# Decay rows spread from DRAM, turned Gram products, sample states as the moving operand and state increments on four row groups

## The chip, the cores and the metric

The kernel runs on one core of one Trainium2 chip. The metric is the device time of one execution in microseconds (us), as the median of several runs. All data is float32.

## What is computed

One inference step of one decoder layer: 256 prompt tokens and 8 sample sequences of 4 tokens (288 tokens in all, model width 2048). RMSNorm, one input projection, two mixers side by side, one output projection, a mixture of 32 experts with top-2 choice, and a gated per-layer embedding. The change lies in mixer B, a gated DeltaNet with 8 heads of width 128. Per head, cut to what matters:

```python
G = jnp.cumsum(g, axis=-1)                                   # log decays, inside a chunk
decay = jnp.exp(jnp.where(causal, G[..., :, None] - G[..., None, :], -jnp.inf))
a_mat = jnp.where(strict, (k * beta[..., None]) @ k.T * decay, 0.0)
m = a_mat + eye                                              # unit lower triangular
u = solve(m, v * beta[..., None]); w = solve(m, k * beta[..., None] * exp(G)[..., None])
qk = q @ k.T * decay
v_new = u - w @ S
o = (q * exp(G)[..., None]) @ S + qk @ v_new
S = S * exp(G[-1]) + (k * exp(G[-1:] - G)[..., None]).T @ v_new
```

Every sample sequence has its own state S (128 x 128) for each head, so 8 of them per head; the outputs hold the new states too.

## The kernel before

The work is written out by hand for each engine, with semaphores between them. A prologue normalises and turns x (hT holds the 288 tokens as columns), then TensorE runs the first four pieces of the input projection and the sums behind the decays (L664 to L688). Then comes the loop over the heads (`head`, in the blocks of SyncE at L396, TensorE at L690, ScalarE at L1287 and VectorE at L1670): seven passes of a loop and a last one written out. After it come the output projection (L841 on), the experts, and the per-layer embedding.

In each head TensorE does two kinds of work. One is the chain of mixer B and of mixer A: turn v of mixer A, turn the old convolution rows (L712) and the new ones (L716), the sums of squares of q and k (L724), turn k and v and multiply q and k with themselves (`tok_mm`, L729 to L740), turn A and the q-k product (L746 to L750), six doubling levels of the triangular inverse (L753 to L788), u and w (L791 to L796), the states (L801 to L806), v_new (L810 to L812), the outputs (L815 to L819), the state increments of the samples (L823 to L825) and the sum of squares of the output (L827). The other kind is filler: `next_head()` puts the next head's input projection in between (96 matmuls of 128 weights by 288 columns), in portions that the list `FILL` fixes by hand, so that TensorE works while VectorE and ScalarE handle the chain. The last head has less filler (`LAST_FILL`): two pieces, and then the first matmuls of the output projection.

In the trace a float32 matmul stands as two MATMUL rows (two passes), and a transpose as one. A form such as 128*32 128x288 is 128 rows by 32 columns of weights, with 288 moving columns.

VectorE builds gcol (L1680), the decay differences dd (L1717), the masked decays DS and DC (L1724 to L1727), Am and QKm (L1730 to L1735), and from the turned Am fourteen masked blocks NT (L1745). It also does the convolution (L1690, L1694), the level updates (L1764 to L1767), eight masked copies Vm of the samples' v_new (L1804) and the new sample states (L1816). ScalarE takes the exponentials (L1323 to L1325), nine scaled copies of k and v (L1328 to L1330) and the copies out of PSUM. SyncE's queue carries all loads and stores of the heads: pieces of 1 MB, small rows per head, the states.

The products of the samples with their states: the state is the stationary operand and eight columns (w and q of one sequence) move past it, eight times per head.

Of the kernel before, what the change touches and what calls it, by code (L numbers as in the profile page):

```python
# [9 lines left out]
ALU = mybir.AluOpType  # L10
# [42 lines left out]
def _constants():  # L53
# [3 lines left out]
    same = (row // SEQ_LEN) == (col // SEQ_LEN)  # L57
    parts = [("ident", row == col), ("triu", row <= col), ("before", row < col), ("ones", row >= 0 * col),
             ("causal", row >= col), ("strict", row > col),
             ("low0", (row % 2 == 1) & (col == row - 1))]  # L60
    for lev in range(LEVELS):
# [5 lines left out]
              ("seq", row // SEQ_LEN == np.arange(SEQS)[None, :]),  # L67
# [46 lines left out]
def trunk(nc, d, o):  # L114

    ctx = ExitStack()
    with ctx:
# [77 lines left out]
        Dm = w(2, P)
        Ds = w(SAMPLE)
        DS = w(2, P)
        DSs = w(SAMPLE)
        eG = w(TOK)
        qg = w(TOK)  # L200
        Am = w(2, P)
        Ams = w(SAMPLE)
        QKm = w(2, P)
        QKms = w(SAMPLE)
# [10 lines left out]
        XTs = w(SAMPLE)  # L215
# [4 lines left out]
        uTs = w(SAMPLE)  # L220
        WQ = w(SEQS, 2 * SEQ_LEN)
# [3 lines left out]
        vnTs = w(SAMPLE)  # L225
        vns = w(P)
        Vm = w(SEQS, P)
# [3 lines left out]
        csT = w(3, P)  # L231
        stt = w(3, P)
# [15 lines left out]
        DC = w(2, P)  # L248
        DCs = w(SAMPLE)
# [49 lines left out]
        def gate_sig(q, t):  # L299
            if t == 2:  # L300
# [15 lines left out]
                 "tok_cp", "A_r", "AT_mm", "QKT_r", "NT_r", "W_r", "dS_mm", "W_T", "WT_r", "Wrep", "WTs_r", "ln_d",  # L316
                 "ln_sq", "vn_r", "mixA_mm", "mixA_r", "uw_mm", "uw_cp", "WQ_r", "S1_mm", "S1_r", "SQ_mm", "wS_mm",
                 "vn1_r", "vnT_r", "vnTT", "Vm_r", "vns_r", "o_mm", "S2_r", "Sn_r", "os_p", "os_r", "osq_r", "oss_mm", "rn_r", "or_r",
# [34 lines left out]
        def _(sp):  # L353
# [12 lines left out]
            def load_state(cols):  # L366
                for s in range(3):
                    sp.dma_start(stt[0:SEQS * PAD, s, :], conv_in[:, bass.ds(cols[s], P)]).then_inc(E["st_ld"], 16)
# [11 lines left out]

            for s in range(PIECES):
                load_piece(s, piece_col[s])
# [13 lines left out]
            def head(h, pieces, inputs):  # L396
# [19 lines left out]
                for s in range(3):  # L416
                    sp.dma_start(cv_p[:, bass.ds(c[s], P)], csT[0:PAD, s, :]).then_inc(E["cs_st"], 16)
                    sp.dma_start(cv_s[:, bass.ds(c[s], P)], csT[PAD:PAD + SEQS * PAD, s, :]).then_inc(E["cs_st"], 16)
# [161 lines left out]
        def _(pe):  # L580
# [106 lines left out]
            mm(ps[0:SAMPLE, 3, 16:24], C("btriu", SAMPLE), g[0:SAMPLE, 2, :])  # L687
            mm(ps[0:SAMPLE, 3, 40:48], C("ball", SAMPLE), g[0:SAMPLE, 2, :]).then_inc(dec["prep_mm"], 1)  # L688

            def head(h, fill):  # L690
# [38 lines left out]
                for t, (off, n) in enumerate(TILES):  # L729
                    pe.transpose(ps[0:n, 5, t * P:(t + 1) * P], qk[:, 1, off:off + n], C("ident"))  # L730
                    pe.transpose(ps[0:n, 6, t * P:(t + 1) * P], qkvT[:, 2, off:off + n], C("ident"))  # L731
                for t in range(2):
                    kt, qt = qk[:, 1, t * P:(t + 1) * P], qk[:, 0, t * P:(t + 1) * P]
# [3 lines left out]
                kt, qt = qk[:, 1, PROMPT:TOK], qk[:, 0, PROMPT:TOK]  # L737
                mm(ps[0:SAMPLE, 4, 0:SAMPLE], kt, kt)
                mm(ps[0:SAMPLE, 4, SAMPLE:2 * SAMPLE], qt, kt)
# [1354 lines left out]
```

## Time and profile before

| | |
|---|---|
| median of 3 runs | 1909.12 us (1908.06 to 1911.35) |
| profiled execution | 1911.12 us, span 1909.3 us |
| TensorE busy (matmul) | 1800.0 us, 94% |
| VectorE busy | 556.5 us, 29% |
| ScalarE busy | 388.0 us, 20% |
| mean DMA rate over the span | 278 GB/s |
| one pass of the head loop | 71.69 us |

The span is the time between the first and the last instruction of the profiled execution; the 1.8 us beside it are launch and end. Busy is time in which an engine executed an instruction. The heads take from 67 us to about 645 us. From about 810 us on the DMA engines move some 427 GB/s with almost no break, until 1740 us.

### The profile page before, as it was taken

How to read it: one execution, taken by the hardware profiler on the slowest of the kernel's cores; microseconds unless marked ns; L12 is line 12 of the kernel's file. 1: busy time of each engine (PE TensorE's matmuls, PEld its weight loads, DVE VectorE, ACT ScalarE, POOL GpSimd, SP SyncE). 2: the span in 40 equal slices, each digit the busy share in tenths (PEclk: the TensorE clock that was granted, in tenths of full speed). 3: DMA queues.
4: the chain of work that ended last, by engine and by line, in shares of the span. 5: the costliest groups of instructions: out<-in, count | busy, mean ns of one | idle time of the engine just before them, and what ended most of it. 6: DMA issues, size and time to landing. Idle time of an engine off the chain costs nothing.

```text
span 1909.3 us, 22816 instructions
## 1 busy us (share of the span) xinstructions
PE 1800.0 (94%) x8060; PEld 933.9 (49%) x8060; DVE 556.5 (29%) x1811; ACT 388.0 (20%) x922; POOL 19.5 (1%) x37
## 2 busy tenths in 40 slices
PE   7999999999998999999999999999999999999998
PEld 4777777777775433433333333333333333334333
DVE  2334434434434200321323213232132311224113
ACT  1424524524523111311000111001010010002103
POOL 0000000000000000000000000000000000000000
PEclk9999999999999999999999999999999999999999
DMA  8333433433404461599999999999999999999401
GB/s 253 100 95 102 126 94 103 124 94 104 124 28 149 152 250 73 199 419 428 427 428 427 427 427 427 427 427 427 428 426 427 425 427 425 424 424 384 168 22 50
DMA packets 208462, 519.92 MB, mean 272 GB/s; under 512 B 18664, under 2 KB 139488, under 8 KB 157152
## 3 DMA queue, kind: packets, MB, share of 16 engines
q1 hardware_dynamic: 198160, 513.83, 69.0%
q0 software_dynamic: 2304, 4.86, 0.7%
q10 hardware_dynamic: 7968, 0.83, 0.3%
q8 instruction: 19, 0.31, 0.1%
q14 instruction: 11, 0.09, 0.0%
HBM read 519.14 MB, written 12.26 MB: 278 GB/s over the span
## 4 chain that ended last, share of the span: by engine, by line
PE 79%; DMA 17%; DVE 2%; ACT 1%; issue 1%; SPq 0%; DVEq 0%; ACTq 0%
PE ps L582 75%; DMA ring<-in_w_down_dram 17%; PE ps L585 3%; DMA x<-in_x_sample_dram 0%; PE ps L1082 0%; ACT hb L1210 0%; ACT ring L1210 0%; SPq L477 0%; DMA pp_rows<-hb 0%; DVE ring L1694 0%; PE ps L710 0%; PE ps L730 0%; DVE ring L1745 0%; PE ps L731 0%; DVE x L2011 0%
## 5 line engine op out<-in xcount | busy, mean ns | idle before, releaser
L582 PE MATMUL ps<-ring,hT 128*64 128x512 f32 x2048 | 457.0, 596 | 25.6 <-DMA ring<-in_w_up_dram 25.6
L582 PE MATMUL ps<-hT,ring 128*128 128x288 f32 x1536 | 410.1, 414 | 0.0
L582 PE MATMUL ps<-ring,mixT 128*64 128x512 f32 (+2 forms) x1408 | 365.6, 598 | 35.9 <-DMA ring<-in_w_down_dram 25.6
L582 PEld LDWEIGHTS ps<-hT,ring 128*128 128x128 f32 x1536 | 283.3, 192 | 70.4 <-issue 0.5
L582 PEld LDWEIGHTS ps<-ring,hT 128*64 128x64 f32 x2048 | 145.7, 137 | 308.4 <-issue 305.8
L582 PEld LDWEIGHTS ps<-ring,mixT 128*64 128x64 f32 (+2 forms) x1408 | 124.8, 144 | 240.2 <-issue 238.3
L582 PE MATMUL ps<-ring,hb 128*128 128x512 f32 (+2 forms) x512 | 143.7, 512 | 0.0
L582 PE MATMUL ps<-mixT,wpT 128*128 128x512 f32 (+1 forms) x384 | 130.1, 601 | 0.0
L582 PEld LDWEIGHTS ps<-ring 128*128 128x128 f32 (+3 forms) x880 | 115.7, 186 | 29.0 <-DVE ring L1767 7.9
L582 PE MATMUL ps<-ring 128*128 128x128 f32 (+3 forms) x880 | 123.8, 272 | 1.7 <-DVE ring L1754 1.6
L1210 ACT ACTIVATE ring<-ps 128x256 f32<-128x256 f32 (+5 forms) x176 | 47.5, 310 | 294.4 <-PE ps L582 256.8
L582 PEld LDWEIGHTS ps<-ring,hb 128*128 128x128 f32 (+1 forms) x512 | 65.2, 170 | 78.1 <-issue 78.0
L1210 ACT ACTIVATE hT<-ps 128x512 f32<-128x512 f32 (+1 forms) x76 | 37.5, 494 | 322.6 <-PE ps L582 237.0
L2007 DVE TENSOR_TENSOR x<-x,ps 128x512 f32<-128x512 f32 x128 | 88.0, 687 | 24.8 <-PE ps L582 23.2
L1958 DVE TENSOR_SCALAR hT<-ps,gJ 128x128 f32<-128x128 f32 x128 | 35.9, 343 | 194.4 <-PE ps L585 194.4
L582 PEld LDWEIGHTS ps<-mixT,wpT 128*128 128x128 f32 (+1 forms) x384 | 49.8, 162 | 78.7 <-issue 53.6
L1999 DVE COPY mixT<-ps 128x512 f32<-128x512 f32 x16 | 11.1, 691 | 215.4 <-PE ps L582 215.4
L1210 ACT ACTIVATE wpT<-ps 128x288 f32<-128x288 f32 (+2 forms) x19 | 7.2, 383 | 318.4 <-PE ps L1082 313.9
L1210 ACT ACTIVATE mixT<-ps 128x512 f32<-128x512 f32 x32 | 19.1, 597 | 223.7 <-PE ps L582 223.7
L1210 ACT ACT_TABLE_LOAD x47 | 60.3, 1283 | 2.4 <-DVE sc L1662 1.0
L1764 DVE TENSOR_TENSOR ring<-ring,ps 128x256 f32<-128x256 f32 x40 | 16.9, 422 | 121.9 <-PE ps L582 121.9
L1986 DVE TENSOR_TENSOR mixT<-hT,ps 128x256 f32<-128x256 f32 x16 | 6.7, 421 | 133.3 <-ACT hT L1210 133.3
(248 smaller groups left out, 1096.7 us busy)
## 6 DMA issues: line engine op xcount, KB each, us to landing
ring<-in_w_gate_dram SPq DMA_DIRECT2D x128, 1024.0 KB, 22.5
ring<-in_w_up_dram SPq DMA_DIRECT2D x128, 1024.0 KB, 24.4
ring<-in_w_down_dram SPq DMA_DIRECT2D x128, 1024.0 KB, 22.0
ring<-in_w_in_dram SPq DMA_DIRECT2D x48, 1024.0 KB, 5.6
ring<-in_w_out_dram SPq DMA_DIRECT2D x16, 1024.0 KB, 11.0
ring<-in_w_ple_gate_dram SPq DMA_DIRECT2D x16, 1024.0 KB, 13.3
hb<-in_state_delta_dram SPq DMA_DIRECT2D x8, 512.0 KB, 5.2
out_dram<-hb SPq DMA_DIRECT2D x8, 512.0 KB, 3.7
```

The costliest lines, as they stand in the source:

```text
L582: return pe.matmul(out, lhsT, rhs, start=start, stop=stop)
L585: return pe.transpose(out, in_, C("ident", n, n))
L1210: return act.activation(out, in_, func, **kw)
L1764: tt(X[:, :, :], X[:, :, :], two(6), ALU.subtract)
L1958: last = ts(xT[:, k, :], ps[:, j, i * P:(i + 1) * P], gJ[:, k:k + 1], None, ALU.mult)
L1986: tt(hx[:, 0], sg[:, 0], up(6), ALU.mult).then_inc(M["h0"], 1)
L1999: cp(yx[:, 512:1024], ps[:, 1, :]).then_inc(M["y_v"], 1)
L2007: tt(xs, xs, ps[:, ((4, 5), (6, 7), (0, 1), (2, 3))[n][t], :], ALU.add).then_inc(M["add"], 1)
```

## The change

It does seven things.

1. **Decay rows.** The prologue makes the running sums of the decays and the betas also as rows (8 heads x 288 tokens), stores them to DRAM (`gb_rows`), and for every head one DMA spreads the head's two rows over all 128 partitions (`Gb`). VectorE waits for it at the start of the head and makes the differences dd and dT there; gcol and the three matmuls that spread it are gone.
2. **Turned Gram products.** One matmul per tile multiplies k with k and q together (256 moving columns). VectorE masks the result straight in the turned form (NTa, QKT), so that Am, QKm and their six transposes with the wait `A_r` and `AT_mm` are gone. The blocks NT are masked for both tiles at once, and those of later levels between the levels.
3. **Convolution rows.** Three transposes of the old rows become one, and three of the new rows become one.
4. **Sample states as the moving operand.** 32 zero-padded columns of w and q of a sequence are the weights, and the state's 128 columns move; the eight matmuls go to four column groups of the array.
5. **v_new of the samples** is made by two matmuls that accumulate (one with the inverse, laid out four times, one that picks w's rows and negates them) instead of u for the samples, a subtraction and a transpose. The samples' q part is picked by one more matmul into the output, instead of an addition on VectorE.
6. **Increments on four row groups.** k and v_new of the samples stand at four partition groups of 32; VectorE makes two masked copies instead of eight, and four matmuls of 256 columns, one per row group, write to four PSUM banks.
7. **Places.** The sum of squares of the output goes to bank 7 and waits for S2; the increments wait for the output's copy `os_p`. The copies `kd` of the samples and their decays hold all 128 partitions.

The diff, cut to its core:

```diff
@@ sync
+            def load_rows(h):
+                sp.dma_start(Gb.rearrange("p a n -> p (a n)"), gb_rows[bass.ds(h, 1), :].to_broadcast([P, 2 * TOK])
+                             ).then_inc(E["gb_ld"], 16)
@@ sync, after the first AHEAD pieces
+            sp.wait_ge(dec["prep_v"], 4)
+            sp.dma_start(gb_rows, gb_stage.rearrange("p a n -> p (a n)")).then_inc(E["gb_st"], 16)
+            sp.wait_ge(E["gb_st"], 16)
+            load_rows(0)
@@ sync, head, after load_gate(h1)
+                    load_rows(h1)
@@ tensor, prologue
-            mm(ps[0:SAMPLE, 3, 16:24], C("btriu", SAMPLE), g[0:SAMPLE, 2, :])
-            mm(ps[0:SAMPLE, 3, 40:48], C("ball", SAMPLE), g[0:SAMPLE, 2, :]).then_inc(dec["prep_mm"], 1)
+            for r in range(0, P, 32):
+                mm(ps[r:r + 32, 3, 16:24], C("btriu", SAMPLE), g[0:SAMPLE, 2, :])
+                last = mm(ps[r:r + 32, 3, 40:48], C("ball", SAMPLE), g[0:SAMPLE, 2, :])
+            beta = pre[:, 3]
+            for t in range(2):
+                mm(ps[0:HEADS, 3, 64 + t * P:64 + (t + 1) * P], g[:, t, :], C("triu"))
+                mm(ps[0:HEADS, 2, t * P:(t + 1) * P], beta[:, t, :], C("ident"))
+            mm(ps[0:HEADS, 3, 64 + PROMPT:64 + TOK], g[0:SAMPLE, 2, :], C("btriu", SAMPLE))
+            mm(ps[0:HEADS, 2, PROMPT:TOK], beta[0:SAMPLE, 2, :], C("ident", SAMPLE, SAMPLE)).then_inc(dec["prep_mm"], 1)
@@ tensor, head
-                for s in range(3):
-                    last = tr(ps[:, 2, s * 24:(s + 1) * 24], stt[0:SEQS * PAD, s, :], SEQS * PAD)
-                last.then_inc(E["st_T"], 1)
+                tr(ps[:, 2, 0:72], stt[0:72, :], 72).then_inc(E["st_T"], 1)
                 pe.wait_ge(E["cs_r"], h1)
-                for s in range(3):
-                    last = tr(ps[0:27, 4, s * P:(s + 1) * P], cs[:, s, :], P)
-                last.then_inc(E["cs_T"], 1)
+                tr(ps[0:81, 4, 0:P], cs[:, :, :].rearrange("p s c -> p (s c)"), P).then_inc(E["cs_T"], 1)
...
+                        for r in range(0, P, 32):
+                            mm(ps[r:r + 32, 5, t * P:(t + 1) * P], qk[:, 1, PROMPT:TOK], C("ident"))
...
-                    mm(ps[:, 7, t * P:(t + 1) * P], kt, kt)
-                    mm(ps[:, 7, 256 + t * P:256 + (t + 1) * P], qt, kt)
-                    mm(ps[:, 2, t * P:(t + 1) * P], gcol[:, t, :], C("triu"))
+                    mm(ps[:, 7, t * 256:(t + 1) * 256], qk[:, 1, t * P:(t + 1) * P], qk[:, :, t * P:(t + 1) * P])
-                mm(ps[0:SAMPLE, 4, 0:SAMPLE], kt, kt)
-                mm(ps[0:SAMPLE, 4, SAMPLE:2 * SAMPLE], qt, kt)
-                mm(ps[:, 2, PROMPT:TOK], gcol[0:SAMPLE, 2, :], C("btriu", SAMPLE)).then_inc(E["tok_mm"], 1)
+                mm(ps[0:SAMPLE, 4, 0:2 * SAMPLE], qk[:, 1, PROMPT:TOK], qk[:, :, PROMPT:TOK]).then_inc(E["tok_mm"], 1)
                 next_head()
-
-                pe.wait_ge(E["A_r"], h1)
-                pe.wait_ge(E["tok_cp"], h1)
-                pe.wait_ge(E["D_r"], h1)
-                for t in range(2):
-                    tr(ps[:, 5, t * P:(t + 1) * P], Am[:, t, :], P)
-                    tr(ps[:, 6, t * P:(t + 1) * P], QKm[:, t, :], P)
-                tr(ps[0:SAMPLE, 5, 256:256 + SAMPLE], Ams[0:SAMPLE, :], SAMPLE)
-                tr(ps[0:SAMPLE, 6, 256:256 + SAMPLE], QKms[0:SAMPLE, :], SAMPLE).then_inc(E["AT_mm"], 1)
                 next_head()
...
-                mm(ps[:, 5, PROMPT:TOK], vb[0:SAMPLE, 2, :], XTs[0:SAMPLE, :])
...
                 for b in range(SEQS):
-                    last = mm(ps[:, 2, b * 8:(b + 1) * 8], Sold[:, b, :], WQ[:, b, :])
+                    g = 32 * (b % 4)
+                    last = mm(ps[g:g + 32, 2, 0:P], WQ[:, 32 * b:32 * b + 32], Sold[:, b, :], b < 4, b >= 4)
...
-                pe.transpose(ps[0:SAMPLE, 5, 0:P], vnTs, C("ident")).then_inc(E["vnTT"], 1)
+                pe.wait_ge(E["SQ_r"], h1)
+                mm(ps[:, 5, 0:P], XTs4[0:SAMPLE, :, :], vb[0:SAMPLE, 2, :], True, False)
+                mm(ps[:, 5, 0:P], C("pick_w"), SQs, False, True).then_inc(E["vns_mm"], 1)
...
-                mm(ps[:, 4, PROMPT:TOK], vns[0:SAMPLE, :], QKTs[0:SAMPLE, :]).then_inc(E["o_mm"], 1)
+                mm(ps[:, 4, PROMPT:TOK], vns[0:SAMPLE, :], QKTs[0:SAMPLE, :], True, False)
+                mm(ps[:, 4, PROMPT:TOK], SQs, C("pick_q"), False, True).then_inc(E["o_mm"], 1)
                 next_head()
                 pe.wait_ge(E["Vm_r"], h1)
-                for q in range(2):
-                    last = mm(ps[:, 5 + q, :], kd[0:SAMPLE, 2, :], Vm[0:SAMPLE, 4 * q:4 * q + 4, :])
+                pe.wait_ge(E["os_p"], h1)
+                for r in range(4):
+                    rows = slice(32 * r, 32 * r + 32)
+                    last = mm(ps[:, 3 + r, 0:2 * P], kd[rows, 2, :], Vm[rows, 0:2, :])
@@ vector, prologue
+            cp(gb_stage[:, 0, :], ps[0:HEADS, 3, 64:64 + TOK])
+            cp(gb_stage[:, 1, :], ps[0:HEADS, 2, 0:TOK])
@@ vector, head
-                for t, (_, n) in enumerate(TILES):
-                    ts(gcol[0:n, t, :], C("ones", n), hs[0:n, t, 0:1], None, ALU.mult)
+                v.wait_ge(E["gb_ld"], snap(h * 16 + 16))
+                for out, sample, clip in ((dd, dds, ALU.max), (dT, dTs, ALU.min)):
+                    for t in range(2):
+                        ts(out[:, t, :], Gb[:, 0, t * P:(t + 1) * P], hs[:, t, 1:2], 0.0, ALU.subtract, clip)
+                    last = ts(sample[0:SAMPLE, :], Gb[0:SAMPLE, 0, PROMPT:TOK], hs[0:SAMPLE, 2, 1:2], 0.0, ALU.subtract, clip)
+                last.then_inc(E["dd_r"], 1)
...
+                        for r in range(3, -1, -1):
+                            tt(XTs4[0:SAMPLE, r, :], XTs[0:SAMPLE, :], ps[0:SAMPLE, 7, 256:256 + SAMPLE], ALU.subtract)
```

## Rows read from the trace of the kernel before

**Rows 1.** The page: the chain that ended last, by engine.

```profile
PE 79%; DMA 17%; DVE 2%; ACT 1%; issue 1%; SPq 0%; DVEq 0%; ACTq 0%
```

**Rows 2.** Busy times by stretch, one loop pass: PE, PEld, DVE, ACT, POOL, clock, DMA, GB/s.

```profile
286.27:357.96 71.69, 70.40 (x367) 55.81 (x365) 30.19 (x127) 27.48 (x68) 0.00 (x0) 1.00 0.39 107
```

**Rows 3.** Timeline of TensorE, that pass: start, length, group, rows, idle before.

```profile
287.47 0.51 PE L585 MATMUL ps<-cst,ring 128*27 128x128 f32 x3 [0.71 <-DVE ring L1688]
...
295.09 1.14 PE L582 MATMUL ps<-ring,cst 128*128 128x288 f32 x4
...
300.43 0.27 PE L730 MATMUL ps<-cst,ring 128*128 128x128 f32 x1
...
302.52 0.31 PE L582 MATMUL ps<-ring 128*32 128x32 f32 x4
302.76 0.40 PE L582 MATMUL ps<-cst,ring 32*128 32x32 f32 x2
303.09 6.09 PE L582 MATMUL ps<-hT,ring 128*128 128x288 f32 x24
309.02 0.76 PE L585 MATMUL ps<-cst,ring 128*128 128x128 f32 x6
309.71 4.63 PE L582 MATMUL ps<-hT,ring 128*128 128x288 f32 x18
...
318.68 0.64 PE L582 MATMUL ps<-ring 128*128 128x128 f32 x4
...
338.21 1.61 PE L582 MATMUL ps<-ring 128*128 128x128 f32 x12
...
342.24 1.85 PE L582 MATMUL ps<-ring,hb 128*128 128x8 f32 x16
343.94 2.19 PE L582 MATMUL ps<-hT,ring 128*128 128x288 f32 x8
...
346.19 0.27 PE L812 MATMUL ps<-cst,ring 128*32 128x128 f32 x1
...
351.47 1.98 PE L582 MATMUL ps<-hb,ring 32*128 32x512 f32 x4
```

**Rows 4.** Timelines of VectorE and ScalarE, the same pass.

```profile
285.93 0.67 DVE L1680 TENSOR_SCALAR ring<-cst,hs 128x128 f32<-128x128 f32 x3
...
318.15 0.40 DVE L1767 TENSOR_TENSOR ring<-ring,ps 128x256 f32<-128x256 f32 x1
...
292.78 1.93 ACT L1210 ACTIVATE ring<-ring 128x768 f32<-128x768 f32 x5 [2.98 <-DVE ring L1694]
```

**Rows 5.** Timeline of TensorE, the prologue and the start of head 0.

```profile
46.45 2.15 PE L582 MATMUL ps<-hT,wab 128*32 128x288 f32 x32
...
64.87 1.17 PE L582 MATMUL ps<-pre,cst 128*128 128x8 f32 x12
67.30 0.56 PE L710 MATMUL ps<-cst,hb 128*128 128x128 f32 x3 [1.26 <-DVE pre L1657]
...
70.34 0.84 PE L585 MATMUL ps<-cst,ring 128*27 128x128 f32 x3 [2.05 <-DVE ring L1688]
```

**Rows 6.** The DMA view, whole span: issue, size of one, median us to landing.

```profile
hb<-in_state_delta_dram SPq DMA_DIRECT2D x8, 512.0 KB, 5.2
...
hb<-in_b_s_dram SPq DMA_DIRECT2D x8, 64.0 KB, 2.6
...
out_dram<-hb SPq DMA_DIRECT2D x8, 16.0 KB, 1.4
```

**Rows 7.** Busy times by stretch at the start of head 0, columns as in rows 2.

```profile
67.00:70.00 3.00, 1.00 (x6) 0.66 (x6) 2.44 (x13) 1.60 (x3) 0.00 (x0) 0.62 1.05 305
70.00:73.00 3.00, 2.66 (x8) 2.00 (x9) 2.92 (x9) 1.76 (x2) 0.00 (x0) 0.50 0.06 15
```

**Rows 8.** TensorE's waits in the last head and after it: us, times, longest.

```profile
PE ps L582 <- DVE ring L1754: 1.6, 1, 1.6
PE ps L585 <- DVE ring L1735: 1.4, 1, 1.4
```

More of the change, by code:

```diff
@@ L191, in trunk @@
         qk = w(2, TOK)
-        gcol = w(3, P)
+        Gb = w(2, TOK)
         dd = w(2, P)
         dds = w(SAMPLE)
[L195 to L198, printed above, removed]
+        dT = w(2, P)
+        dTs = w(SAMPLE)
+        DL = w(2, P)
+        DLs = w(SAMPLE)
         eG = w(TOK)
         qg = w(TOK)
[L201 to L204, printed above, removed]
+        EB = w(2, P)
+        EBs = w(SAMPLE)
+        NTa = w(2, P)
+        NTas = w(SAMPLE)
         kbg = w(3, P)
@@ L214, in trunk @@
         Xs = w(SAMPLE)
-        XTs = w(SAMPLE)
+        XTs4 = w(4, SAMPLE)
+        XTs = XTs4[:, 0, :]
         T1 = w(2, P)
@@ L219, in trunk @@
         wT = w(2, P)
-        uTs = w(SAMPLE)
-        WQ = w(SEQS, 2 * SEQ_LEN)
+        WQ = w(272)
+        WQ_cols = WQ.rearrange("p (h x) -> p h x", h=2)[:, :, 0:P].rearrange("p h (g c) -> p h g c", g=4)
+        SQs = w(P)
         S1 = w(P)
@@ L1668, in _, with both @@
             n_before = ch.n
+            def both(name):
+                return C(name).unsqueeze(1).to_broadcast([P, 2, P])
             def head(h, loop):
@@ L1722, in head @@
                 tt(qg, qk[:, 0, :], eG, ALU.mult)
+                st(out=DL[:, :, :], in0=dd[:, :, :], scalar=-1.0, in1=both("low0"), op0=ALU.mult, op1=ALU.mult)
+                st(out=DLs[0:SAMPLE, :], in0=dds[0:SAMPLE, :], scalar=-1.0, in1=C("low0", SAMPLE, SAMPLE), op0=ALU.mult,
+                   op1=ALU.mult)
+                tt(CT[:, :, :], dT[:, :, :], both("triu"), ALU.mult)
+                tt(CTs[0:SAMPLE, :], dTs[0:SAMPLE, :], C("btriu", SAMPLE), ALU.mult)
+                tt(EB[:, :, :], dT[:, :, :], Gb[:, 1, 0:PROMPT].rearrange("p (t n) -> p t n", t=2), ALU.mult)
@@ L1743, in head, with masked @@
-                for lev in range(LEVELS):
-                    for t in range(2):
-                        last = tt(NT[:, lev, t, :], ps[:, 5, t * P:(t + 1) * P], C(f"mt{lev}"), ALU.mult)
+                def masked(lev):
+                    return tt(NT[:, lev, :, :], NTa[:, :, :], both(f"mt{lev}"), ALU.mult)
                 for lev in range(2):
-                    last = tt(NTs[0:SAMPLE, lev, :], ps[0:SAMPLE, 5, 256:256 + SAMPLE], C(f"mt{lev}", SAMPLE, SAMPLE), ALU.mult)
+                    masked(lev)
+                    last = tt(NTs[0:SAMPLE, lev, :], NTas[0:SAMPLE, :], C(f"mt{lev}", SAMPLE, SAMPLE), ALU.mult)
@@ L1748, in head @@
                 ch(last)
+                tt(X[:, :, :], X[:, :, :], both("ident"), ALU.add)
+                tt(Xs[0:SAMPLE, :], Xs[0:SAMPLE, :], C("ident", SAMPLE, SAMPLE), ALU.add)
                 ch.wait()
-                for t in range(2):
-                    tt(X[:, t, :], X[:, t, :], C("ident"), ALU.add)
-                    st(out=XT[:, t, :], in0=NT[:, 0, t, :], scalar=-1.0, in1=C("ident"), op0=ALU.mult, op1=ALU.add)
-                tt(Xs[0:SAMPLE, :], Xs[0:SAMPLE, :], C("ident", SAMPLE, SAMPLE), ALU.add)
+                st(out=XT[:, :, :], in0=NT[:, 0, :, :], scalar=-1.0, in1=both("ident"), op0=ALU.mult, op1=ALU.add)
@@ L1802, in head @@
                 v.wait_ge(E["vns_r"], h1)
-                for b in range(SEQS):
-                    last = ts(Vm[0:SAMPLE, b, :], vns[0:SAMPLE, :], C("seq", SAMPLE)[:, b:b + 1], None, ALU.mult)
+                for i in range(2):
+                    last = ts(Vm[:, i, :], vns, C("seq")[:, i:i + 1], None, ALU.mult)
                 last.then_inc(E["Vm_r"], 1)
-                v.wait_ge(E["os_p"], h1)
-                os4 = sq4(oS[:, PROMPT:TOK])
-                tt(os4, os4, SQ[:, :, SEQ_LEN:], ALU.add).then_inc(E["os_r"], 1)
+                v.wait_ge(E["o_mm"], h1)
                 v.wait_ge(E["s2_st"], snap(h * 16 + 1))
```

125 lines of the change are left out of this document (60 added, 65 removed).

## The prediction

> **What bounds the kernel now.** I read the chain that ended last first: 79% of the span is TensorE, 17% a DMA [rows 1]. The DMA share lies in the experts, which the change does not touch. So the question is who ends last in the heads. The busy times of one loop pass answer it: TensorE 70.40 of 71.69 us, VectorE 30.19, ScalarE 27.48, granted clock 1.00 (2.4 GHz), 107 GB/s [rows 2]. TensorE is the bound, with 1.3 us idle per pass, all at its start: 0.71 us of them for VectorE's convolution rows [rows 3]. In such a pass a microsecond taken from TensorE's own list is a microsecond saved, and one taken from VectorE is worth nothing while the filler covers it. All later work hangs on TensorE's progress, so what the heads give is passed on whole.
>
> **How I price TensorE.** The timeline gives starts, and the distance between starts counts: a group's length overlaps the next one by some 0.15 us (16 rows from 342.24 to 343.94 are 1.70 us, length 1.85) [rows 3]. Three prices: a row with 128 weight columns and up to 128 moving ones costs 0.107 us (those 16 rows have 8 columns and cost no less than the 128-column ones, 0.11); 288 moving columns cost 0.247 us (24 rows from 303.09 to 309.02), so 256 cost 0.215; and a change of shape to 32 weight columns or to 32 rows, and back, costs about 0.1 us each time. The last I read from 302.52 to 303.09: six tiny rows take 0.57 us, of which 4 x 0.03 and 2 x 0.107 are their own; the rest is spent at the three changes around them.
>
> **TensorE, part by part, for one pass.**
> - Products of q and k: before, from 300.43 to 303.09, 2.66 us [rows 3]. After: four transposes of 128 columns and one of v's sample columns 0.54; k's sample rows to four column groups, 8 rows; four rows of 256 columns 0.86; two small rows 0.12; four changes of shape 0.4. The eight rows are priced by the one place where four column groups work already: 32 rows of 288 columns in 2.15 us, 0.065 each against 0.247 alone [rows 5], so four run side by side; 8 rows of 128 columns are then 2 x 0.107. Sum 2.13, saved 0.5.
> - The turned A and q-k: 309.02 to 309.71, saved 0.7 [rows 3].
> - u of the samples: 2 of 12 rows at 338.21, saved 0.2 [rows 3].
> - Sample states: 1.70 us now [rows 3]. After 16 rows of 128 columns on four column groups, as in [rows 5]: 4 x 0.107, two changes 0.2, so 0.63. Saved 1.07. Bounds: side by side 1.07; one after the other 16 x 0.107 + 0.2, a loss of 0.2.
> - v_new: one row of 0.11 (346.19) [rows 3] becomes four rows and two changes, 0.63. Lost 0.5.
> - Outputs: two more rows. Lost 0.2.
> - Increments: four rows of 512 columns, length 1.98, 1.83 on the path [rows 3]. After eight rows of 256 columns on four row groups. No row of this trace has row groups. One after the other: 8 x 0.215 + 0.2 = 1.9, a loss of 0.1. Side by side: 2 x 0.215 + 0.2 = 0.63, a gain of 1.2. If the weight loads (128 columns each) go one by one it is 8 x 0.107 + 0.2 = 1.06. I take 0.8, near the side-by-side end, since the nearest rows are the column groups [rows 5]. Saved 1.0.
> - The transposes of the convolution rows: 0.22 less at 287.47 [rows 3], but see the next part.
>
> Sum: 0.5 + 0.7 + 0.2 + 1.07 - 0.5 - 0.2 + 1.0 = 2.8 us per pass.
>
> The Trainium skill (TensorEngine Tiling (Array Packing), Tiling Modes) says that a change of the tiling mode drains the array; that speaks against this change, which adds four or five of them to a head. The rows agree with a price, and it is the 0.1 us used above. The skill (TensorE: Matmul & The Clock Gate, Why this matters for your kernels) gives 3.07 times for four row groups of 512 columns; by it the increments would take an estimated 1.8 / 3.07 = 0.6 us, the sum would be 3.0 us; no row here shows it.
>
> **What the other engines do to that.**
> - Head start. VectorE makes three gcol columns in 0.67 us before it takes the old convolution rows [rows 4]. After it makes four of 128 columns and two of 32, some 1.0 to 1.1 us, at the same place, and it then comes 0.2 us later than the transposes did. TensorE's one transpose instead of three gives that back. Net 0.
> - Sums of squares: ScalarE's squares end at 292.78 + 1.93 = 294.71 [rows 4], TensorE asks at 295.09 [rows 3]. VectorE's 0.2 us later eats half of the 0.38; no new wait, or one of 0.1.
> - Level 1: VectorE ends XT at 318.55 [rows 4], TensorE starts level 2 at 318.68 [rows 3]. Three more 32x32 operations at 0.1 us stand ahead of XT. A wait of 0.2 us is new.
> - The inverse's start: the decays are ready before the products now, and VectorE needs some 5 us for masks after the exponentials. Its cover is the two filler portions of 24 and 18 rows, 10.3 us together [rows 3]; without them TensorE would stand about 3 to 5 us. Nine copies on ScalarE hide there too.
> - Copies of the state products on ScalarE (SQs) and of v_new have a filler portion of 8 rows, 2 us, each against 0.5. The increments' new wait for the output's copy has the same cover. Nothing.
> - The row load per head (295 KB) stands on SyncE's queue behind the gate loads and ahead of piece 3. It lands in 3 to 5 us [rows 6] and is needed some 18 us later; pieces are six slots ahead. Nothing.
>
> So 2.6 us per pass, 8 passes 20.8 us.
>
> **The last head** has little filler. TensorE waits there 1.4 us for Am (L1735) and 1.6 us for the first NT (L1754) [rows 8]. The first wait and its transposes go; the second had 14 masks in front, now four operations for both tiles, beside 11 filler matmuls (5.4 us) in one stretch. Both go: 3.0 us.
>
> **The prologue pays.** Before, the sums end near 66.0 and the head starts at 67.30; the convolution rows are turned at 70.34 [rows 5]. After: 24 more small rows on TensorE, at 0.03 to 0.107 (0.7 to 2.6; I take 1.4); two copies of 288 columns on VectorE, 0.45 each by gcol's rate, 0.9. Then SyncE issues the store (0.4) which lands in 1.4 as the 16 KB store does, sees it and issues the spread load (0.5), which lands in 2.6 to 5.2 [rows 6]; 2.8 by the broadcast row of 64 KB, which it is nearest to in kind. The last piece's transfer is out of the way by 70 us (305 GB/s, then 15) [rows 7]. Then VectorE's six operations and the convolution rows, 1.7. That is 67.0 + 2.3 + 5.1 + 1.7 = 76.1 against 70.34: 5.7, less 0.2 for two transposes, 5.5 us of a standing TensorE. VectorE's other preparations lie inside it. Bounds 3.5 to 9. The granted clock falls to 0.50 (1.2 GHz) behind today's wait already [rows 7], so its half-speed stretch is paid now as well and I add nothing. The constants grow by 8%, loaded where TensorE waits for x; nothing.
>
> **Sum.** 20.8 + 3.0 - 5.5 = 18.3 us. The profiled execution took 1911.12, so 1892.8; it was 2.0 above the median 1909.12, so about 1890.8 for a median.
>
> **Rivals.**
> - A. The row groups don't work side by side, or the weight loads keep them apart. For it: no row shows them, and each needs 128 columns of weights. The gain of 1.0 becomes -0.1: 8.8 us less, 1899.6. Chance 0.13.
> - B. The way through DRAM is dearer: the store waits behind the piece on the queue, the spread of one row to 128 partitions is slow, and the sq wait opens. 5.5 becomes 9 and each pass loses 0.1 to 0.2: 1895.5. Against it [rows 7]. Chance 0.15.
> - C. Neither group form works side by side (the change doesn't do what it says): states -0.2 and increments -0.1 instead of 1.07 and 1.0, 19 us less: 1910, no change. Against it: [rows 5]. Chance 0.04.
> - D. Slower: changes of shape at full drain. Between two shapes a matmul's whole length, 0.3 to 0.6 us and not 0.1, stands on the path, at the ten or so changes of a head. 10 x 0.3 more is 3 us a pass, 24 us in all, and it ends at 1915; it decides from 0.23 us more per change, where the gain of 18.3 is gone. The rows at 302.52 to 303.09 speak against it [rows 3]; what could still bring it is that row groups change more than the rows here do. Chance 0.03.
>
> **How the numbers follow.** The forecast has 0.65; its own range, from the bounds of the increments (+1.6 us over all heads if best), the prologue (-2 to +3.5) and the state products, is 1885 to 1896. With B and most of A the range is 1884 to 1899. About 0.2% (3.8 us) is what a measurement of this kernel can tell from no change. Faster: 0.65 + 0.13 + 0.15 = 0.93; same 0.04; slower 0.03.
>
> **What would show it.** In the profile after: a loop pass of about 69.0 us; the stretch of state products near 0.65 us with starts in fours; increments under 1.1 us; no row of L585 between the two filler portions; a wait of 0.2 us before level 2; in head 0 a TensorE wait of 7 to 8 us that ends with VectorE's convolution rows, and before it VectorE waiting for a DMA; in the last head no wait of the kinds L1735 and L1754. Wrong would be: a pass above 70 us, a new wait in the middle of a pass, or a head 0 that starts after 80 us.

## The result, and the profile after

| | before | after |
|---|---|---|
| median | 1909.12 us (1908.06 to 1911.35), 5 runs | 1896.07 us (1893.70 to 1900.93), 5 runs |
| profiled execution | 1911.12 us, span 1909.3 us | 1893.70 us, span 1891.9 us |
| TensorE busy | 1800.0 us | 1780.5 us |
| VectorE busy | 556.5 us | 541.6 us |

The ratio of the two is 0.9937, 95% interval [0.9926, 0.9949]. The change makes the kernel faster by 13.05 us. The forecast was 18.3 us and 1890.8 us; the time lies inside the range of 1884 to 1899 us, 5.3 us above the forecast. The profiled execution is the fastest of the five, so the profiled pair differs by 17.4 us and not by 13.05; the end of this part says where the 17.4 us lie.

The page after: the chain that ended last, by engine. It answers to [rows 1]; TensorE still bounds, and the DMA share is the experts' as before.

```profile
PE 77%; DMA 18%; DVE 3%; issue 1%; ACT 1%; SPq 0%; DVEq 0%; ACTq 0%
```

Busy times by stretch of the kernel after, two head passes (columns as in [rows 2]), and one microsecond near the start of the first and of the second:

```profile
145.00:216.04 71.04, 69.22 (x357) 53.91 (x357) 28.19 (x112) 27.63 (x67) 0.00 (x0) 0.98 0.41 112
216.04:285.39 69.35, 67.53 (x357) 52.84 (x357) 28.19 (x112) 27.53 (x67) 0.00 (x0) 1.00 0.43 115
...
146.00:147.00 1.00, 1.00 (x4) 0.72 (x3) 1.00 (x3) 0.95 (x1) 0.00 (x0) 0.50 1.16 331
...
217.00:218.00 1.00, 1.00 (x5) 0.76 (x5) 1.00 (x3) 0.99 (x1) 0.00 (x0) 1.00 1.16 336
```

There are two kinds of pass now, and that is the main finding. With as many matmuls in both, one takes 71.04 us and the other 69.35, where before every such pass took 71.7 [rows 2]. The difference lies in the first microseconds: the granted clock is 0.50 (1.2 GHz) there in the first kind, and 1.00 (2.4 GHz) in the second. A loss of 1.69 us each time, in four of the six loop passes that follow head 0.

TensorE's waits from 60 to 660 us of the kernel after (us, times, longest):

```profile
PE ps L603 <- DVE hb L1714: 14.5, 8, 6.6
...
PE ps L752 <- DVE ring L1739: 0.5, 1, 0.5
```

Both waits of [rows 8] are gone. The first row shown is the wait for the convolution rows, 8 times: 6.6 us in head 0, about 1.2 us in six passes and 0.8 in the last head, where it was 0.71 us a pass before [rows 3]. The last row, ahead of the transposes of k, is not new: before, a wait of 2.1 us for VectorE (L1713) stood at the same place of the last head (TensorE's L730), and the part on the prediction comes back to it.

TensorE's timeline of the kernel after, the pass that begins at 216.04 us with the head start ahead of it (start, length, group, rows, idle before), the places that answer to [rows 3]:

```profile
214.25 0.54 PE L735 MATMUL ps<-cst,hb 128*128 128x128 f32 x3 [0.58 <-ACT hb L1226]
214.63 0.23 PE L603 MATMUL ps<-cst,hb 72*128 72x72 f32 x1
216.04 0.34 PE L603 MATMUL ps<-cst,hb 128*81 128x128 f32 x1 [1.19 <-DVE hb L1714]
216.23 7.54 PE L600 MATMUL ps<-hT,ring 128*128 128x288 f32 x30
...
228.94 0.27 PE L752 MATMUL ps<-cst,ring 128*128 128x128 f32 x1
...
231.13 10.45 PE L600 MATMUL ps<-hT,ring 128*128 128x288 f32 x42
241.42 0.78 PE L600 MATMUL ps<-ring 128*128 128x128 f32 x6
...
244.85 1.24 PE L600 MATMUL ps<-hT,ring 128*128 128x288 f32 x4
246.15 0.71 PE L600 MATMUL ps<-ring 128*128 128x128 f32 x4
...
269.65 0.65 PE L600 MATMUL ps<-hb,ring 128*32 128x128 f32 x16
270.22 2.21 PE L600 MATMUL ps<-hT,ring 128*128 128x288 f32 x8
272.26 0.38 PE L600 MATMUL ps<-hb,ring 128*128 128x128 f32 x2
272.58 0.48 PE L600 MATMUL ps<-ring 32*128 32x128 f32 x2
272.99 0.49 PE L600 MATMUL ps<-ring,cst 128*128 128x128 f32 x2
273.32 2.11 PE L600 MATMUL ps<-hT,ring 128*128 128x288 f32 x8
...
278.71 0.71 PE L600 MATMUL ps<-hb,ring 32*128 32x256 f32 x8
279.36 0.75 PE L600 MATMUL ps<-ring,cst 128*128 128x288 f32 x2
```

Read by the distance between starts, this gives every term of the forecast for a pass:

| term, us per pass | forecast | measured | from |
|---|---|---|---|
| products of q and k | 0.5 | 0.47 | 2.66 before, 228.94 to 231.13 is 2.19 |
| turned A and q-k | 0.7 | 0.80 | both portions in one, 10.29; before 11.09 with the transposes |
| u of the samples | 0.2 | 0.23 | 1.54 before, 1.31 |
| sample states | 1.07 | 1.13 | 1.70 before, 0.57 |
| v_new | -0.5 | -0.73 | 0.33 before, 272.26 to 273.32 is 1.06 |
| outputs | -0.2 | -0.25 | 1.09 before, 1.34 |
| increments | 1.0 | 1.26 | 1.91 before, 0.65 |
| level 1 | -0.2 | -0.23 | 1.07 before, 244.85 to 246.15 is 1.30 |
| head start | 0 | -0.10 | wait 0.48 longer, transposes 0.38 shorter (0.23 ahead of the wait, 0.15 behind it) |
| clock | 0 | 0 or -1.69 | the two kinds of pass |

The terms without the clock add up to 2.58 against a forecast of 2.6; the pass itself is 2.35 shorter (71.70 to 69.35), the missing 0.2 being spread in steps of 0.1 (the 30 rows take 7.54 instead of 7.44).

Head 0 of the kernel after, timelines of TensorE, of VectorE and of SyncE (issues):

```profile
62.41 1.21 PE L600 MATMUL ps<-pre,cst 128*128 128x8 f32 x24
...
66.79 0.70 PE L735 MATMUL ps<-cst,hb 128*128 128x128 f32 x3 [1.99 <-DVE pre L1676]
...
74.17 0.50 PE L603 MATMUL ps<-cst,hb 128*81 128x128 f32 x1 [6.56 <-DVE hb L1714]
```

```profile
72.44 0.48 DVE L1704 TENSOR_SCALAR ring<-ring,hs 128x128 f32<-128x128 f32 x2 [3.90 <-DMA ring<-gb_rows]
```

```profile
66.47 0.32 SPq L404 DMA_DIRECT2D gb_rows<-hb  x1
68.97 0.35 SPq L391 DMA_DIRECT2D ring<-gb_rows  x1
```

The store is issued at 66.47 and seen 2.50 us later; the load takes 3.47 us from its issue to VectorE's first use. From the sums to the convolution rows it is 62.41 to 74.17, 11.76 us; before it was 64.87 to 70.34, 5.47 us [rows 5]. So the prologue costs 6.3 us.

**The account, from the profiled pair.** Seven passes, convolution rows to convolution rows: 503.83 us before (70.34 to 574.17), 493.17 after, 10.7 saved. The last head up to its increments: 68.22 before, 61.82 after, 6.4 saved, and 1.3 for the increments. The prologue: 6.3 lost. From the sums to the end of the heads' increments that is 12.0 us, near the 13.05 of the medians. The other 5.4 us of the profiled pair lie outside of this part: 2.5 us ahead of the sums, where x landed 0.9 us earlier and the first 64 rows took 16.94 us instead of 18.53, and 2.9 us behind the heads. No run tells whether any of those 5.4 us belongs to the change.

### The profile page after: what moved, and what is told of

It reads as the page before. It is cut to its first block, busy times and chain, and to the rows that moved or that the text cites. A ratio compares the mean times of both kernels' runs of the same rounds, so it can differ in the third digit from the quotient of the medians.

```text
span 1891.9 us, 22679 instructions
## 1 busy us (share of the span) xinstructions
PE 1780.5 (94%) x8020; PEld 913.0 (48%) x8020; DVE 541.6 (29%) x1693; ACT 389.1 (21%) x922; POOL 19.4 (1%) x37
## 4 chain that ended last, share of the span: by engine, by line
PE 77%; DMA 18%; DVE 3%; issue 1%; ACT 1%; SPq 0%; DVEq 0%; ACTq 0%
PE ps L600 74%; DMA ring<-in_w_down_dram 17%; PE ps L603 3%; DVE hb L1836 1%; PE ps L1098 0%; DMA x<-in_x_sample_dram 0%; DVE ring L1704 0%; SPq L495 0%; ACT ring L1226 0%; DVE ring L1720 0%; DMA pp_rows<-hb 0%; DVE ring L1789 0%; ACT hb L1226 0%; PE ps L756 0%; DMA ring<-gb_rows 0%
## 5 line engine op out<-in xcount | busy, mean ns | idle before, releaser
L600 PE MATMUL ps<-hT,ring 128*128 128x288 f32 x1536 | 414.7, 419 | 0.0
L600 PEld LDWEIGHTS ps<-hT,ring 128*128 128x128 f32 x1536 | 287.7, 194 | 74.5 <-issue 1.9
L600 PEld LDWEIGHTS ps<-ring 128*128 128x128 f32 (+3 forms) x752 | 100.4, 185 | 28.5 <-DVE ring L1790 10.2
L600 PE MATMUL ps<-ring 128*128 128x128 f32 (+5 forms) x752 | 110.8, 279 | 0.6
L600 PEld LDWEIGHTS ps<-ring,hb 128*128 128x128 f32 (+2 forms) x448 | 59.7, 166 | 81.3 <-issue 78.5
L1226 ACT ACTIVATE ring<-ps 128x256 f32<-128x256 f32 (+3 forms) x136 | 37.8, 316 | 243.0 <-PE ps L600 243.0
L1226 ACT ACTIVATE hb<-ps 128x288 f32<-128x288 f32 (+2 forms) x75 | 28.1, 376 | 120.0 <-PE ps L600 67.2
```

The lines of the kernel that those rows point to most:

```text
L600: return pe.matmul(out, lhsT, rhs, start=start, stop=stop)
L1226: return act.activation(out, in_, func, **kw)
```

## The experiments

The forecast's reasons to test were: the head start, which the forecast had put at nothing; the clock; the row groups (rival A) and the column groups. A cold pass below is one whose 30 filler rows behind the wait take about 9.2 us instead of 7.5; the count is over the six passes after head 0, in the profiled execution.

**The decay block behind the layer norm.** In the changed kernel VectorE makes the decay differences, 1.1 us of work, before the convolution rows that TensorE waits for. Here it makes them after `ln_d`, where nobody waits soon (in the expectations below: e1_decays_late, or e1).

```diff
@@ vector, head
-                v.wait_ge(E["gb_ld"], snap(h * 16 + 16))
-                for out, sample, clip in ((dd, dds, ALU.max), (dT, dTs, ALU.min)):
...
                 v.wait_ge(E["st_T"], h1)
@@ vector, head, after ln_d
+                v.wait_ge(E["gb_ld"], snap(h * 16 + 16))
+                for out, sample, clip in ((dd, dds, ALU.max), (dT, dTs, ALU.min)):
...
```

> The changed kernel with one block moved: VectorE waits for the decay rows and makes dd and dT behind the layer norm's subtraction (ln_d) instead of at the start of the head. Theory (the block ahead of the convolution rows lengthens TensorE's idle at a head's start from 0.71 to 1.2 us, and behind the longer idle the granted clock falls to 0.5 for some 3.6 us in part of the passes, 1.7 us each; and head 0 waits for the trip through DRAM there): the wait for the convolution rows falls to 0.7 to 0.8 us, no pass with a half-speed stretch, the 30 filler rows take 7.4 to 7.5 us in every pass; in head 0 TensorE's wait falls from 6.6 to about 3 us. Passes of 68.9 us; 6 x 0.45 + 4 or 5 x 1.7 + 3.5, so 13 to 15 us less: about 1882. Rival (the half-speed stretches come from something else in the change: less busy array under column and row groups, or the row load on the DMA engines): the clock still falls in about half of the passes, and only 6 to 7 us are won: about 1889.

Measured: 1886.39 us, ratio to before 0.9880 [0.9864, 0.9895], 9.7 us better than the changed kernel. TensorE's timeline of head 0 and of the start of a pass (68.88 us):

```profile
63.81 1.21 PE L600 MATMUL ps<-pre,cst 128*128 128x8 f32 x24
...
70.76 0.50 PE L603 MATMUL ps<-cst,hb 128*81 128x128 f32 x1 [1.97 <-DVE hb L1708]
...
210.94 0.34 PE L603 MATMUL ps<-cst,hb 128*81 128x128 f32 x1 [0.71 <-DVE hb L1708]
211.12 7.54 PE L600 MATMUL ps<-hT,ring 128*128 128x288 f32 x30
```

The wait is back at 0.71 us, no pass is cold, and head 0's wait falls from 6.56 to 1.97 us, because VectorE waits for the row load behind the work that TensorE needs. Then the prologue costs 1.5 us instead of 6.3 (63.81 to 70.76 is 6.95). So of what the change loses there and by the clock, nearly all comes from the place of one block. The expected 13 to 15 us did not come whole: by the trace the seven passes give 8.6 us and the prologue 4.8, but the last head takes back 1.5, and outside of these parts the profiled execution is 3.2 us slower than that of the changed kernel, so that the profiled pair differs by 8.7 us and the medians by 9.7.

**Old convolution rows ahead of the wait for mixer A's v**, on top of that. The transpose of the old rows needs nothing that is late, and VectorE starts from it.

```diff
@@ tensor, head
+                pe.wait_ge(E["st_ld"], snap((h + 1) * 48))
+                tr(ps[:, 2, 0:72], stt[0:72, :], 72).then_inc(E["st_T"], 1)
                 pe.wait_ge(piece_ev, snap(h * PIECES + (VA + 1)))
-                pe.wait_ge(E["st_ld"], snap((h + 1) * 48))
...
-                tr(ps[:, 2, 0:72], stt[0:72, :], 72).then_inc(E["st_T"], 1)
```

> e1 and in addition TensorE turns the old convolution rows before it waits for mixer A's v, so VectorE can take them sooner. Theory: the wait for the convolution rows falls from 0.75 to 0.1 to 0.3 us, a pass from 68.9 to 68.4, 4 us less than e1 over all heads: about 1878. Rival (TensorE's start is not what orders VectorE there, or the sums of squares then wait for ScalarE by as much): same as e1, with a new wait ahead of the ones product.

Measured: 1879.72 us, 0.9849 [0.9835, 0.9862]. The wait is 0.25 us, no pass is cold, a pass takes 68.28 us (209.19 to 277.47), 0.60 less than in the run above. The median fell by 6.7 us, where 4 were expected and eight times 0.60 would be 4.8; no run explains the rest.

**The level 1 copies off the path**, on top of both. VectorE writes the inverse's sample part once, makes the full XT, and only then copies the three others in one operation.

```diff
@@ vector, level 1
-                        for r in range(3, -1, -1):
-                            tt(XTs4[0:SAMPLE, r, :], XTs[0:SAMPLE, :], ps[0:SAMPLE, 7, 256:256 + SAMPLE], ALU.subtract)
+                        ch(tt(XTs[0:SAMPLE, :], XTs[0:SAMPLE, :], ps[0:SAMPLE, 7, 256:256 + SAMPLE], ALU.subtract))
...
+                    if lev == 1:
+                        ch.wait()
+                        cp(XTs4[0:SAMPLE, 1:4, :], XTs[0:SAMPLE, :].unsqueeze(1).to_broadcast([SAMPLE, 3, SAMPLE]))
```

> e2 and in addition, at level 1, only the one needed 32x32 subtraction stands ahead of XT on VectorE, and the three further copies of XTs are made behind it by one copy. Theory (those three operations make TensorE wait 0.2 us ahead of level 2): the distance from the start of the 4 filler rows to level 2 falls from 1.30 to 1.07 us, a pass by 0.2, 1.7 us in all: about 1878. Rival (TensorE is held there by something else): same as e2, distance 1.30.

Measured: 1875.33 us (1874.35 to 1876.32), 0.9822 [0.9809, 0.9834]: 20.7 us better than the changed kernel and 33.7 better than the one before. TensorE's timeline:

```profile
238.99 1.24 PE L600 MATMUL ps<-hT,ring 128*128 128x288 f32 x4
240.06 0.64 PE L600 MATMUL ps<-ring 128*128 128x128 f32 x4
```

The step to level 2 takes 1.07 us again, as before the change. The forecast's 0.2 us for it was right. The median fell by 4.4 us, of which eight times 0.23 us are 1.8; the rest is open, so the total does not confirm the size, the step does. This is the best version of the study.

**Idle VectorE work in the kernel before**, to lengthen the wait without anything else of the change: three operations, then eight, then four (e9_before_delay12).

```diff
@@ vector, head (3, 8 or 4 times; their result is not used)
+                for i in range(3):
+                    ts(NT[:, 3 + i // 2, i % 2, :], C("ones"), hs[:, 0, 0:1], None, ALU.mult)
```

> The kernel before with three more 128-column operations of VectorE (0.6 us, results unused) at the start of each head, ahead of the convolution rows; nothing else. Theory: the idle ahead of the convolution rows goes from 0.71 to 1.1 to 1.2 us and the clock falls behind it in part of the passes as in the changed kernel: passes of 72.1 us or 73.9 us, 8 x 0.45 + 3 to 6 x 1.7, so 9 to 14 us more: 1918 to 1923. Rival (the length of that idle is not the cause): all passes 72.1 us, clock 1.00, 1913.

> The same with eight operations (1.6 us). Theory: idle of 2.1 to 2.2 us, a half-speed stretch behind it in every pass: 8 x 1.45 + 7 x 1.75, 24 us more: about 1933. Rival: 8 x 1.45 alone, 1921, clock 1.00.

> The kernel before with four idle VectorE operations at the start of each head, so that TensorE's wait for the convolution rows is about 1.2 us, as long as in the changed kernel. Two theories. (a) The length of the wait decides: the 30 filler rows behind it take 9.1 us or so in about half of the passes, 7.44 in the others, and the whole is 7 x 0.5 + 3 to 4 x 1.7 = 9 to 10 us above before, some 1918. (b) It is the other work around the wait in the changed kernel (fewer transposes on TensorE, the row spread on the queues) that makes the clock fall, and a wait of 1.2 us alone does it as seldom as one of 1.0 us did (one pass of seven): 3.5 + 0 to 1.7 us, some 1913 to 1914.

Measured: with waits of 1.01 us 1909.37 us, 1.0006 [0.9997, 1.0015]; with 1.21 us 1916.71 us (1912.77 to 1918.08), 1.0036 [1.0024, 1.0048]; with 1.99 us 1924.04 us, 1.0085 [1.0069, 1.0100]. Cold passes: one, one, and four of six. Two neighbouring passes with the 1.99 us wait:

```profile
220.93 0.51 PE L585 MATMUL ps<-cst,ring 128*27 128x128 f32 x3 [1.99 <-DVE ring L1690]
221.28 7.44 PE L582 MATMUL ps<-hT,ring 128*128 128x288 f32 x30
...
293.90 0.51 PE L585 MATMUL ps<-cst,ring 128*27 128x128 f32 x3 [1.98 <-DVE ring L1690]
294.25 9.13 PE L582 MATMUL ps<-hT,ring 128*128 128x288 f32 x30
```

The first expectation missed by 8.6 us and more (its wait also fell short of the 1.1 us it had aimed at), the second by 9: a longer wait costs the clock more often, but even 2 us not in every pass.

One trace per run is not enough for the counts here, since executions of one kernel differ. The mean granted clock on record for every run helps. With the 1.01 us wait, the profiled execution, with one cold pass, has a mean clock of 0.995; six of the other nine have 0.996 at 1908.44 to 1909.48 us, and three have 0.993 or 0.994 at 1912.61 to 1914.26 us. With the 1.21 us wait, the profiled execution (0.995, 1913.41 us) is one of two at that clock; the other five have 0.991 to 0.993 and take 1915.81 to 1918.08 us, 2.4 to 4.7 us more. With four cold passes, the 1.99 us wait has 0.992. So five of the seven executions with the 1.21 us wait very likely had one to three cold passes more than the one in the trace, as theory (a) of the last expectation says, whose time of 1918 us is also nearer to the median. That is argued from clock and time; those executions have no trace.

**The same wait in the changed kernel by other work.** The decay block stays late, and idle operations take its old place: four of them (e10_late_delay12), then six.

```diff
@@ vector, head (4 or 6 times; their result is not used)
+                for i in range(4):
+                    ts(NT[:, 3 + i // 2, i % 2, :], C("ident"), hs[:, 0, 0:1], None, ALU.mult)
```

> The changed kernel with the decay block moved late (as in e1_decays_late), and in its old place four idle VectorE operations that bring the wait back to about 1.2 us, without the wait for the row load and without the block's own work there. If the standing TensorE alone decides, the passes are as in the changed kernel: the 30 filler rows take 9.2 us in about half of the passes and 7.54 in the others, pass 69.4 or 71.0, and the time is 3.5 + 4 x 1.7 = 10 us above the 1886.4 of e1_decays_late, near 1896. If the block itself matters, the rows stay at 7.54 and the time is near 1890.

> As e10_late_delay12 with six idle VectorE operations instead of four, since there the wait only reached 0.81 us; each further one adds 0.2 us, so it is now about 1.2 us. If the standing TensorE alone decides, the rows behind the wait are slow (9.2 us instead of 7.54) in part of the passes: in three to four of six if it is as in the changed kernel, 1884.4 + 2.8 + 5 to 7 us, 1892 to 1894; in one of six if it is as in e9_before_delay12, near 1889 to 1891. If the decay block itself or its wait for the row load matters, none is slow and the time is near 1887.

Four missed their aim, since VectorE had a wait of its own there to fill (0.72 us for TensorE's transposes, in the run with the late block): TensorE's wait grew only to 0.81 us, none of the passes was cold, 1884.37 us. That says nothing on 1.2 us, but it puts one more point at the harmless end. Six gave 1894.82 us, 0.9923 [0.9906, 0.9939]. Two passes of it:

```profile
143.30 0.34 PE L603 MATMUL ps<-cst,hb 128*81 128x128 f32 x1 [1.23 <-DVE hb L1710]
143.58 9.23 PE L600 MATMUL ps<-hT,ring 128*128 128x288 f32 x30
...
214.45 0.34 PE L603 MATMUL ps<-cst,hb 128*81 128x128 f32 x1 [1.19 <-DVE hb L1710]
214.63 7.54 PE L600 MATMUL ps<-hT,ring 128*128 128x288 f32 x30
```

Four of six passes are cold, and they are the same four as in the changed kernel (cold, warm, cold, cold, warm, cold). So neither the block nor its wait for the row load is needed; a longer standing TensorE is enough in this kernel. From 0.81 to 1.19 us of wait the time rises by 10.5 us, of which about 3 are the wait itself.

**The wait filled with useless transposes** in the changed kernel, which lengthens nothing that VectorE does.

```diff
@@ tensor, head, ahead of the wait for cs_r
+                for i in range(8):
+                    tr(ps[:, 4, P:2 * P], C("ident"), P)
```

> The changed kernel with eight more transposes of a constant (0.86 us of TensorE, results unused) in the 1.2 us in which it waits for the convolution rows; nothing else. Theory (the clock falls because TensorE stands still too long at the head's start): the wait shrinks to 0.3 to 0.4 us at the same length of the stretch, no pass has a half-speed stretch, the 30 filler rows take 7.5 us in all, so 4 to 5 x 1.7 us less in spite of more work: about 1889. Rival (the fall has another cause, the state of VectorE or the DMA traffic): some 30-row stretches still take 9.2 us, 1896.

Measured: 1892.24 us (1892.15 to 1893.69), 0.9915 [0.9902, 0.9927], where about 1889 was expected.

```profile
214.76 1.04 PE L603 MATMUL ps<-cst 128*128 128x128 f32 x8
216.10 0.34 PE L603 MATMUL ps<-cst,hb 128*81 128x128 f32 x1 [0.31 <-DVE hb L1716]
216.34 7.54 PE L600 MATMUL ps<-hT,ring 128*128 128x288 f32 x30
```

TensorE does more and the convolution rows come no earlier, yet the kernel is 3.8 us faster and no pass is cold. Together with the six idle operations this shows TensorE's standing time as what lowers the clock in this kernel, from both sides: add standing time without the block and the clock falls, take standing time away with the block in place and it stays.

**The increments on one row group again**, with the eight masked copies on VectorE that belong to it, the rest as in the changed kernel.

```diff
@@ tensor
-                for r in range(4):
-                    rows = slice(32 * r, 32 * r + 32)
-                    last = mm(ps[:, 3 + r, 0:2 * P], kd[rows, 2, :], Vm[rows, 0:2, :])
+                for q in range(2):
+                    last = mm(ps[:, 5 + q, :], kd[0:SAMPLE, 2, :], Vm[0:SAMPLE, 4 * q:4 * q + 4, :])
```

> The changed kernel with the increments as before: eight masked copies on 32 partitions and two matmuls of 512 columns on one row group, all else as changed. Theory (four row groups run side by side, gain 1.27 us per head): the increments take 1.91 us again, 8 x 1.27, 10 us more: 1906. Rival (the shorter increments only moved the wait to the head's start): 1896 to 1899, with a shorter wait for the convolution rows.

Measured: 1906.28 us, 0.9981 [0.9972, 0.9989], 10.2 us above the changed kernel.

```profile
284.43 1.98 PE L600 MATMUL ps<-hb,ring 32*128 32x512 f32 x4
```

The next row starts at 286.33, so the stretch is 1.90 us again; eight times 1.25 us is 10.0, and the median rose by 10.2. The four row groups work side by side, and rival A is refuted.

**The column groups in another order**: two matmuls on the same column group one after the other, instead of four on four and then four more.

```diff
@@ tensor
-                for b in range(SEQS):
+                for b in (0, 4, 1, 5, 2, 6, 3, 7):
```

> The changed kernel with the eight state products in the order 0, 4, 1, 5, 2, 6, 3, 7, so that two neighbours use the same column group; nothing else. Theory (the gain comes from four column groups working side by side, and products run in their order): the stretch of 16 rows grows from 0.57 to 0.9 to 1.1 us, 3 to 4 us in all, 1899 to 1900. Rival (the gain comes from 32 weight columns instead of 128 alone): same stretch, no difference.

Measured: 1895.95 us, 0.9940 [0.9926, 0.9954], as the changed kernel.

```profile
269.49 0.67 PE L600 MATMUL ps<-hb,ring 128*32 128x128 f32 x16
270.09 1.24 PE L600 MATMUL ps<-hT,ring 128*128 128x288 f32 x4
```

The stretch is 0.60 us instead of 0.57. The loss that was expected did not come: the order within a set hardly matters. This is what the expectation's rival had forecast (narrow weights alone make the gain), so this run does not show that the column groups work side by side. A place of the changed kernel that has narrow weights and nothing beside them speaks against that rival:

```profile
645.72 1.04 PE L600 MATMUL ps<-wab,cst 128*32 128x512 f32 x2
646.70 4.70 PE L600 MATMUL ps<-ring,mixT 128*128 128x512 f32 x16
```

Two rows with 32 weight columns and 512 moving ones take 0.98 us there, 0.49 each with the changes of shape, no less than rows with 128 weight columns (eight from 651.82 to 655.25, 0.43 each). The 16 state rows of 128 moving columns take 0.57 us together, 0.036 each: a quarter of the columns at less than a tenth of the time. Why the order makes no difference stays open.

## Why the prediction was right or wrong

- **TensorE's list: right.** 2.8 us per pass, less 0.2 for level 1, against 2.35 to 2.58 measured. Behind the sum two sizes were off and cancelled, which is luck. The increments save 1.26 us and not 1.0: they take 0.65 us and not 0.8, less than the 8 x 0.107 that their weight loads would take one by one, and the old ones stood 1.91 us on the path, where the forecast had read 1.83. The Trainium skill (TensorE: Matmul & The Clock Gate, Why this matters for your kernels) gives 3.07 times for four row groups; the trace agrees nearly, with 1.91 / 0.65 = 2.9. v_new loses 0.73 and not 0.5: its six rows take 1.06 us, 0.42 more than six times 0.107, where two changes of shape at 0.1 us had been counted; the rows don't say why. At the states (0.14 us for two) and the increments (0.22) the price of a change held or was less, so rival D found no place.
- **"Head start ... Net 0": wrong, and the main error.** It had compared work (VectorE 0.2 us later, TensorE's transposes as much shorter) and not the wait that is left. The work was nearly right: counted from TensorE's first transposes, VectorE's convolution rows come at 1.79 us (214.25 to 216.04) instead of 1.55 (285.92 to 287.47), 0.24 later, since its six operations take 1.1 us; the transpose behind the wait is 0.15 shorter, and a pass loses 0.1 us. But the transposes ahead of the wait became 0.23 us shorter, and that only made TensorE stand longer: the wait grew by both, from 0.71 to 1.19 us, and for waits the forecast had no price beyond their length.
- **The clock: looked at in one place only.** The sentence "its half-speed stretch is paid now as well and I add nothing" was about head 0, and there it is right: the 30 rows behind the wait took 9.20 us before and 8.86 after. That a wait inside the loop could bring the same in passes where it had never been seen was not asked. It cost 4 x 1.69 = 6.8 us of the profiled execution. The seven passes gave 10.7 us instead of 18.2, and this is 6.8 of the 7.5 missing. The prediction's own sign of being wrong, a pass above 70 us, did appear: four passes take 71 us.
- **The prologue: in bounds, under-sized.** 6.3 us against 5.5. Set to before's start of the sums, the convolution rows are turned at 76.6 us where the forecast had 76.1: the store took 2.50 us from its issue to being seen, where 1.8 was taken, and the load 3.5 where 3.3 was. The 0.2 us taken off for two transposes lie behind that point and had no place in it. Rival B (9 us and a wait for the sums of squares) did not come. That it need not be paid was missed: with the block late it is 1.5 us.
- **The last head: right in kind, more in size, and by luck.** Both named waits are gone; it gave 7.7 us with the increments against 5.6. The forecast had left out a third wait, 2.1 us ahead of the transposes of k. TensorE's timeline there, before:

```profile
582.54 1.62 PE L582 MATMUL ps<-hT,ring 128*128 128x288 f32 x6
586.21 0.33 PE L730 MATMUL ps<-cst,ring 128*128 128x128 f32 x1 [2.05 <-DVE ring L1713]
...
590.57 3.18 PE L582 MATMUL ps<-hT,ring 128*128 128x288 f32 x12
```

and after:

```profile
575.78 3.09 PE L600 MATMUL ps<-hT,ring 128*128 128x288 f32 x6
579.38 0.33 PE L752 MATMUL ps<-cst,ring 128*128 128x128 f32 x1 [0.52 <-DVE ring L1739]
...
581.64 5.60 PE L600 MATMUL ps<-hT,ring 128*128 128x288 f32 x22
```

The wait is shorter only because the six filler rows ahead of it ran at 1.2 GHz (granted clock 0.50); from the convolution rows to the transposes of k it is 12.04 us in both. The half-speed stretch came earlier and so missed the products of q and k, which took 4.36 us before (granted clock 0.50) and 2.26 after. That is 2.1 us saved where 0.5 was forecast, and the difference of 1.6 is most of what the last head gave above its forecast; it comes from where the low clock fell, not from the change's own work. In the run with the late block it fell on these products again, and they took 1.5 us longer than in the changed kernel.
- **The sum.** 12.0 us by the trace instead of 18.3: 7.5 less from the passes, 0.8 less from the prologue, 2.1 more from the last head. The range held, but it had been made for a dearer prologue and for row groups that don't work; what used it up was a loss by the clock that it did not name, and a gain by the clock in the last head hid part of it. The working of TensorE's list per pass was right to a few tenths.

## What to carry to other kernels

Price a wait of the engine that bounds by what stands behind it too: where TensorE's standing time in a loop grows to about a microsecond (in this kernel 0.81 us cost no clock, 1.01 us sometimes did), look at the granted clock of the next ten microseconds in every pass, not in one. Work whose result nobody needs soon belongs behind the operation that the bounding engine waits for, above all if it waits for a DMA itself; here one moved block was worth 9.7 us, as much as the row groups. Small matmuls of 32 rows or 32 columns pay when four go side by side, at about 0.1 us for each change of shape around them.

## What the runs showed that was not expected

- **A wait costs more than its length, but not each time.** Of six passes, cold ones by the length of the wait: none at 0.25, 0.31, 0.71 and 0.81 us; one at 1.01 and at 1.21 us in the kernel before; four at 1.15 to 1.19 us in the changed kernel, in its variants with the other order, with one row group, and with six idle operations, each time the same four; four at 1.99 us in the kernel before. These are counts of one execution each, and the granted clocks of the other executions with 1.21 us speak for more cold passes than the one. The Trainium skill (TensorE: Matmul & The Clock Gate, A second HAM failure mode: psum-queue depth-cycling) says of a bf16 kernel that short pauses which come often between groups of matmuls make the clock swing; the trace agrees in kind, with two pauses of 0.58 and 1.19 us ahead of a pass of 71.04 us, though here they come once a pass. Why a wait of one length lowers the clock in some passes and not in others stays open; the work between TensorE's two waits at the head start (0.83 us of transposes before, 0.61 after), the length of the pass and the time at which the wait falls were not varied alone.
- **Useless work made a kernel faster**: eight transposes in a wait, 3.8 us.
- **Four row groups overlap their weight loads as well as the matmuls**, 0.65 us for eight rows of 256 columns; for four column groups the order of the products made 0.03 us.
